# Gate units between the samples' attention and the delta-rule tiles: six early and six single in place of four and four

## The reference, cut to what matters

```
proj = x @ w_in            # attention q/k/v, delta-rule q/k/v, z, beta, a, gates (2 x 1024)
h = LN1(alpha * x + Mix(x));   y = LN2(alpha * h + ConvFFN(h))
merged = sigmoid(gates[:, :1024]) * (o_att @ w_att_out) + sigmoid(gates[:, 1024:]) * (o_dn @ w_dn_out)
Mix(x) = merged @ w_o
```

## Time and profile before

| | before |
|---|---|
| median of 3 runs | 2015.96 us |
| lowest, highest | 2013.83, 2017.92 us |
| the profiled execution's own time | 2015.21 us |
| its span | 2012.7 us |
| PE busy | 1863.4 us (93%) |
| DVE, ACT, POOL busy | 895.5, 536.8, 407.3 us (44, 27, 20%) |
| mean granted TensorE clock | 0.974 |

### The profile page before, as it was taken

One profiled execution on the slowest core, in us unless ns is written; L12 is line 12 of the kernel. 1 busy time (PEld: TensorE's weight loads), 2 busy tenths in 40 slices (PEclk: granted clock), 3 DMA queues, 4 the chain that ended last, 5 costly groups with the idle time before them and its releaser, 6 DMA issues.

```text
span 2012.7 us, 34454 instructions
## 1 busy us (share of the span) xinstructions
PE 1863.4 (93%) x13645; PEld 1786.7 (89%) x13645; DVE 895.5 (44%) x1616; ACT 536.8 (27%) x982; POOL 407.3 (20%) x196
## 2 busy tenths in 40 slices
PE   7999999999978889997999969999999999999995
PEld 5999999989867779996899959999999999999994
DVE  2003367783655565554681154442124442134427
ACT  2223334334222223322121063232012221022211
POOL 1221111111311111111122151211122112211224
PEclk9999999999989999998999979999999999999997
DMA  4111112332543344444361101111111111111121
GB/s 173 42 42 40 39 65 81 126 106 96 183 154 119 119 140 140 158 161 138 142 250 42 42 11 42 42 52 42 42 42 48 47 42 42 52 42 42 35 73 74
DMA packets 67882, 169.48 MB, mean 84 GB/s; under 512 B 9016, under 2 KB 39352, under 8 KB 66368
## 3 DMA queue, kind: packets, MB, share of 16 engines
q1 hardware_dynamic: 67072, 167.29, 24.3%
q10 hardware_dynamic: 720, 0.92, 0.1%
HBM read 137.81 MB, written 58.52 MB: 98 GB/s over the span
## 4 chain that ended last, share of the span: by engine, by line
PE 81%; DVE 11%; issue 4%; ACT 2%; DMA 2%; POOL 1%; SPq 0%; DVEq 0%; POOLq 0%; ACTq 0%
PE U L670 56%; PE U L758 6%; PE U L1068 3%; PE B L670 2%; DVE cb L1427 1%; PE B L884 1%; PE B L896 1%; PE B L719 1%; PE B L744 1%; PE B L693 1%; PE B L866 1%; PE B L736 1%; DVE stats L1747 1%; DVE kbT L1606 1%; DVE cc L1802 1%
## 5 line engine op out<-in xcount | busy, mean ns | idle before, releaser
L590 POOL TENSOR_TENSOR wl<-stage,wh 128x1024 fp32r<-128x1024 f32 x127 | 309.0, 2433 | 1217.3 <-ACT wh L1090 1217.3
L670 PE MATMUL U<-xh,wh 128*128 128x344 f32 x1392 | 453.1, 326 | 9.0 <-DVE xl L1806 5.8
L670 PE MATMUL U<-xl,wh 128*128 128x344 f32 x1392 | 446.0, 320 | 0.0
L670 PE MATMUL U<-xh,wl 128*128 128x344 f32 x1392 | 445.8, 320 | 0.0
L670 PE MATMUL U<-hh,wh 128*128 128x344 f32 x1056 | 341.2, 323 | 19.5 <-DVE cc L1802 13.1
L670 PE MATMUL U<-hh,wl 128*128 128x344 f32 x1056 | 338.4, 320 | 0.0
L670 PE MATMUL U<-hl,wh 128*128 128x344 f32 x1056 | 338.3, 320 | 0.0
L670 PEld LDWEIGHTS U<-xh,wh 128*128 128x128 f32 x1392 | 262.8, 189 | 10.4 <-issue 10.4
L670 PEld LDWEIGHTS U<-xh,wl 128*128 128x128 f32 x1392 | 262.9, 189 | 0.0
L670 PEld LDWEIGHTS U<-xl,wh 128*128 128x128 f32 x1392 | 262.7, 189 | 0.0
L670 PEld LDWEIGHTS U<-hh,wh 128*128 128x128 f32 x1056 | 199.3, 189 | 25.5 <-issue 25.5
(11 more groups left out here) (343 smaller groups left out, 2640.4 us busy)
## 6 DMA issues: line engine op xcount, KB each, us to landing
stage<-in_wu SPq DMA_DIRECT2D x126, 512.0 KB, 3.3
out_shift<-in_cache SPq DMA_DIRECT2D x8, 2046.0 KB
dn_scr<-thb SPq DMA_DIRECT2D x16, 516.0 KB, 2.6
gate_scr<-gth SPq DMA_DIRECT2D x16, 516.0 KB, 2.9
gates<-gate_scr SPq DMA_DIRECT2D x8, 1032.0 KB, 5.0
out_shift<-in_cache SPq DMA_DIRECT2D x8, 1022.0 KB
dnin<-dn_scr SPq DMA_DIRECT2D x9, 768.0 KB, 14.9
qkv<-in_xT SPq DMA_DIRECT2D x4, 1032.0 KB, 11.7
```

Source lines behind the costliest of these rows:

```text
L590: nc.gpsimd.tensor_tensor(wl[:, par, :], stage[:, par, :], wh[:, par, :].bitcast(F32), ALU.subtract).then_inc(w_lo, 1)
L670: ins = nc.tensor.matmul(dst, a[:, par, w], b[:, xk, third(j)], start=first and n == 0 and m == 0, stop=last and n == len(ks) - 1 and m == 2)
```

## The change

`EARLY` and `SINGLE` go from 4 to 6, so six gate units are issued in stretch 1, tiles 0 to 5 carry one unit each, and only tiles 6 and 7 carry two (6 + 6 + 4 = 16). The portions in stretch 1 go from 8, 30, 0, 0, 22, 4 and 8 to 8, 36, 1, 1, 30, 4 and 28 quarters; the two new single quarters stand between the steps of the maxima. SP's and POOL's orders are extended for the two further units.

```diff
-EARLY = 4
-SINGLE = 4
+EARLY = 6
+SINGLE = 6
# SP
-            for x in range(EARLY - 1):
+            for x in range(3):
                 load(U_GATE + 3 + x, (x + 1) % 2)
                 gate_out(U_GATE + x, x % 2)
+            load(U_GATE + 6, 0)
             sp.wait_ge(samp_pe, 6)
             sp.dma_start(dcst[:], I["dcst"]).then_inc(dcst_in, 16)
+            gate_out(U_GATE + 3, 1)
+            load(U_GATE + 7, 1)
...
             sp.wait_ge(pad_stored, 16)
             rows_in(0)
-            gate_out(U_GATE + EARLY - 1, (EARLY - 1) % 2)
+            gate_out(U_GATE + 4, 0)
+            gate_out(U_GATE + 5, 1)
# POOL, behind the multiplication of L615
-            low(U_GATE + EARLY, 0)
+            for u in range(U_GATE + 4, U_GATE + EARLY + 1):
+                low(u, u % 2)
# PE
             step(ins)
-            beside.run(30)
+            beside.run(36)
             pe.wait_ge(samp_dve, 1)
...
             step(ins)
+            beside.run(1)
             pe.wait_ge(samp_dve, 2)
...
+            beside.run(1)
             pe.wait_ge(samp_dve, 3)
...
-            beside.run(22)
+            beside.run(30)
             pe.wait_ge(samp_dve, 4)
# ACT
-            beside.run(30)
+            beside.run(38)
             act.wait_ge(samp_pe, 5)
...
-            beside.run(22)
+            beside.run(30)
             beside.run(4)
```

## The result

The changed kernel takes 2022.39 us (median of 20 runs, 2016.38 to 2026.65), the kernel before 2016.21 us in the same comparison (20 runs, 2010.31 to 2021.10). The ratio is 1.0028, with a 95% interval of 1.0019 to 1.0037: 5.6 us slower, between 3.8 and 7.5 (the two medians differ by 6.2). The forecast was no change, + 1.05 us, with a range up to 2021.5; the result is above it. The profiled execution took 2023.31 us, with a span of 2021.3 us.

A forecast was written before the change was run, and what follows sets the result against it. PE bounds the kernel (81% of the chain), partly idle and slow in the samples' attention, full in two-unit tiles. Stretch 1 + 11.85, tiles - 10.8, sum + 1.05: 2017.0 us on the runs' median scale, range 2012.5 to 2021.5.

The forecast's parts named there:

- A quarter at 0.631 us: PE's price per gate quarter at the full clock; 36 more quarters cost 22.7 us.
- The tiles' gift: Tiles 4 and 5 go from two units to one and give back 5.40 us each, together 10.8.
- L792 at + 0.5 and L802 at + 1.0 us: Samples' attention: delays from 36 quarters, then two singles, at the steps called L787 and L795 before: 0.5 and 1.0 us.
- The whole clock from 540 to 565: Samples' attention: with gaps gone, PE's clock stays whole; L801 to L807 take 2.86 us instead of 4.41.
- 20 of the 36 quarters lie beside nothing: Last portion of stretch 1: 20 more quarters cost 12.6 us exposed; 16 find room; tile 0 starts 11.85 us later.
- The port: POOL's low part of unit 5 and DVE's L1504 tie, 18.4 against 18.5 us after L795; losing costs 2.25 us.
- `dcst` keeps its place: SP's queue: `dcst` stays behind step 6, an edit costed at nothing.
- rival 2: Ahead of L801: port lost and clock falls with it, + 4.85 us over the median, 2020.8; chance 0.17.
- the bounds: Attention chain: undelayed takes 1.0 us off; clock falling at both old places adds 2.6, mostly unabsorbed, and 1.55: 3.9.
- Rival 1: Ahead of L801: POOL wins the port and L1504 waits, + 2.25 us, 2019.3; chance 0.24.
- Rival 3: Behind the tiles: clock meets another phase, at most 5 us gained; with fastest tiles 2011; chance 0.13.
- Rival 4: Stretch 1: every added quarter is exposed, + 22.7 - 10.8, 2028 us; given no chance.

The follow-up runs named there:

- experiment 5: Changed kernel cut to five early units and five one-unit tiles, with POOL's low part held for DVE and `dcst`'s queue freed: 2011.97 us, ratio 0.9983.
- Experiment 2: Changed kernel with unit 3's store issued before SP's wait and unit 7's load after `dcst` has landed: 2020.63 us, ratio 1.0025 to the kernel before.
- experiment 1: Changed kernel with POOL's low part of unit 5 held until DVE has finished L1511: 2016.96 us, ratio 1.0012 to the kernel before.
- 10: Changed kernel with POOL's low part of unit 3 held until DVE has its first maxima: 2021.72 us, ratio 1.0028 to the kernel before.
- Experiment 4: Changed kernel with the old portions 30, 0, 0, 22, so all 36 added quarters come last: 2025.55 us, ratio 1.0047 to the kernel before.
- 3: Changed kernel with POOL's low part of unit 5 held for DVE and `dcst`'s queue freed: 2016.14 us, ratio 1.0003 to the kernel before.
- 6: Changed kernel with low-part hold and freed `dcst` queue, tile 0's first transposes moved to after 16 of the last 28 quarters: 2009.44 us, ratio 0.9966.
- experiment 7: Five early units, low-part hold and freed `dcst` queue, tile 0's first transposes after 4 of the last 10 quarters: 2005.78 us, ratio 0.9949.
- experiment 8: Kernel before with only tile 0's first transposes moved, to after 4 of its last 8 quarters: 2010.65 us, ratio 0.9972.
- experiment 9: Kernel before with POOL's low part of unit 3 held until DVE has its first maxima: 2012.27 us, ratio 0.9984.

## Why the prediction was wrong, point by point

**Right.** A quarter at 0.631 us: 11.35 us for 18 in experiment 5. The tiles' gift: 10.8 forecast, 10.84 measured. L792 at + 0.5 and L802 at + 1.0 us: 541.47 and 543.69 less 1.92 are 539.55 and 541.77, against 539.5 and 541.6. The whole clock from 540 to 565, and the two long gaps filled. That 20 of the 36 quarters lie beside nothing.

**The step that failed** is the one called "The port", where I had 18.4 us from L795 to the low part and 18.5 to L1504, called it a tie, and gave the forecast to DVE. After L802 the trace has 562.15 - 543.69 = 18.46 for POOL and 562.32 - 543.69 = 18.63 for DVE. The sizes were right to 0.15 us and their order was right; I should have gone by the order. Both times run from the same PE instruction, which speaks against a toss in each execution, and three of three traces without the hold lost it; three are too few to show that it is always lost. It is worth 2.07 us, which I had as 2.25. This is the largest of the three terms that the forecast left out; without the other two, below, the time would still have been inside the range.

**The edit costed at nothing that wasn't.** "`dcst` keeps its place" looked at the order of issue alone. With a store and a load issued behind it, both half a megabyte, it landed in 4.5 us instead of 3.6, and L820 to the last portion took 2.47 us instead of 1.60: 0.87. Experiment 2 shows the transfer at 3.6 again when they are moved away. Over the twelve traces it took 4.0, 4.0 and 4.5 us in the three that have the two transfers right behind it (experiments 1 and 10 and the changed kernel), and 3.3 to 3.7 in the nine others. Experiment 4 is one of the nine, at 3.3, with the changed kernel's order on SP: there unit 3 ends only in the last portion, and its store was issued 12.3 us later.

**The clock.** I expected that it would fall at L808 if anywhere. In the changed kernel it fell 10 us later, in the last portion, which took 19.27 us instead of 17.7: 1.55 lost, the price that I had given for rival 2 at another place. In experiment 2 it fell at L809. In experiment 1 it fell in the last portion with only the 0.92 us wait left, and in 10 with gaps of 2.23 and 0.94. In 3, 5, 6 and 7, with gaps of 0.16 or 0.17 and of 0.48 to 0.58 us, it didn't fall between 540 us and the start of tile 0. So in these eight traces it fell once in each that had a gap of 0.9 us or more, and in none of the others. The size of a gap alone doesn't decide it, though: experiment 8 passed one of 3.45 us ahead of L801 at the whole clock. Which execution pays at which place, and why, isn't settled. The price of the first fall was mis-sized in the bounds as well: in the kernel before, 16 intervals between matmuls at the half clock (541.10 to 545.85 us) took 4.75 us where they take 2.5 at the whole one, so 2.2 us were lost there and not 2.6, over four quarters and not eight. The sum doesn't use that number.

**The sum again**, with what was measured: 11.85 forecast + 0.17 (L802 later) + 2.07 (port) + 0.13 (DVE's chain to L1511) + 0.27 (L808 to L814 at the whole clock: 3.13, not 2.86) + 0.87 (`dcst`) + 1.55 (clock) = 16.91; measured 16.92. Less 10.84 and the 0.3 by which the other tiles ran shorter is 5.8 in the traces; the times say 5.6.

Rival 2 came nearest, with 2020.8 and a chance of 0.17: its first half was right, its clock fell elsewhere, and it lacked the 0.87 of `dcst`. Rival 1 had the port without the clock. Rival 3 didn't happen: from the transposes issued in the last tile to the end it is 1076.0 us after and 1075.2 before. Rival 4 is experiment 4's arrangement, and the trace of the change excludes it.

**What I hadn't asked:** whether the gap that I wanted to fill was real. Of the 3.14 us ahead of L787, 2 were a lost port (experiment 9), and of the 6.08 ahead of tile 0's second transposes 2.1 were another one (experiment 7). The 16 quarters that found room were counted against a kernel that loses that first contest. Against experiment 9's D of 54.84 us, the repaired change (69.88) costs 15.04, which is 24 quarters: beside a kernel before that has the hold, only 12 of the 36 find room. The change would then be worse by 15.04 - 10.84 = 4.2 us, an estimate; the ratios, 1.0003 and 0.9984, give 3.8.

## What to carry to other kernels

Filling work is free only up to what the gaps hold; with the repairs the first unit moved here gained 3.4 us and the second lost 4 (ratios 0.9983 and 1.0003, each good to about 3 us; the traces give a loss of 11.35 - 5.42 = 5.9 for the second), so move one at a time and look what the last portion stands beside. Before filling a gap, look at what ends it: an instruction of 128 x 80 values that takes two microseconds beside a long one on POOL is a gap that a wait on POOL closes for nothing. And when moved work carries instructions of another engine with it (here the low parts on POOL and three transfers), put their new start times beside the critical chain's; where the two are within a few tenths of a microsecond, hold back the one that nobody waits for, and look what it meets instead: in experiment 7 the low part met a later instruction of DVE and held that one up.

## What the runs showed of the hardware

- DVE and POOL exclude each other for whole instructions even when DVE's is tiny: 8 x 768 values took 3.01 us instead of 0.94, 128 x 80 took 2.24 instead of 0.24, and 128 x 4, a scaling with a single input, 2.30 instead of 0.17. There POOL's lead was 0.17, 0.20 and 0.07 us. In experiment 7 a lead of 0.60 us did the same to 128 x 512 (2.32 instead of 0.69), and in experiment 4, where DVE's addition of 128 x 80 began 0.02 us ahead of POOL, it took 0.24. DVE's reductions did not wait: in the changed kernel one of 128 x 2048 took 2.29 us from 531.11 on, with a low part on POOL from 528.88 to 533.33. The Trainium skill's rule ("SBUF — State Buffer", section "Who interferes with whom") holds in every one of these. For the scaling, which has one input, it is that section's line on the operations that can take both ports, with `tensor_scalar` among them.
- One contest may be decided anew in each execution: L1473 or its like took 0.24 us in four of the ten profiles without a hold, among them some with the same instructions up to that point. It can be only a part of why the kernel before spreads over 13 us: the contest is worth 2.6 us of D, and with the hold the runs still spread over 8.
- One transfer of 480 KB landed in 3.4 to 3.7 us with 768 KB issued behind it (eight traces), in 3.3 with nothing behind it, and in 4.0, 4.0 and 4.5 with two more of half a megabyte in between.
- The granted clock fell while PE was busy: in the changed kernel at about 575 us, 1.8 us after a wait of 1.43 us had ended (573.25) and ten after one of 2.23 (565.38).
